# Attention of a two-layer decoder trunk: keys placed by transfers from a shared tile, their product issued earlier, rotated queries' low parts on GpSimd, two weight strips split in halves

## The chip, the core and the metric

The kernel runs on one core of a Trainium2 chip. The metric is the device time of one execution in microseconds (us). Before the change it is 1211.8 us, the median of three runs (1211.34 to 1211.82).

## What is computed

A trunk of two layers over 512 tokens of width 1024, all in float32. Layer 0 mixes tokens by latent attention, layer 1 by an mLSTM; each is followed by a squared-ReLU MLP of width 4096. The change touches only the attention of layer 0:

```
proj = u @ w_in                                   # 512 (c_q) + 256 (c_kv) + 32 (k_r)
q  = rms_norm(c_q, g_q) @ w_uq                    # 16 heads x (64 plain + 32 rotated)
kv = rms_norm(c_kv, g_kv) @ w_ukv                 # 16 heads x (64 keys + 64 values)
q_r, k_r = rope(q_r), rope(k_r)                   # k_r is shared by all heads
for blk in range(4):                              # 128 queries each
    s = (q_n @ k_n.T + q_r @ k_r.T) * 96 ** -0.5  # causal
    p = softmax(s)
    o = p @ v
h = h + o @ w_o
```

## The kernel before

TensorE takes float32 operands as two parts, a high part (a cast to the matmul type, on ScalarE) and a low part (the difference, on VectorE or GpSimd); a product is three matmuls (high x low, high x high, low x high) for each 128 rows of the contraction. Every engine runs a list written by hand, in order, and waits on semaphores; nothing is reordered. So an instruction that waits holds all that stand behind it on its engine.

The attention runs head by head, 0 to 15. Two heads are a pair (their 64 key or query columns fill 128 rows), four are a group (their rotated 32 columns fill 128). `attention(head)` on TensorE is a list of: transposes of the softmax weights of this head (`turn_p(head, b)`, block b of four), scores of the next head (`scores(head + 1, b)`), pieces of products that make the next heads' queries and keys (`rope_product(g)`, `nope_product(pair)`, `k_product(pair)`), and last `weigh(head)`, the product of values and transposed weights. The other engines follow with lists of their own for each head. On ScalarE: `pt_high` (high part of the transposed weights, four), `v_high`, `o_second` (moves half of the head's output), a `split` of a weight strip, `exp(head + 1, b)`. On VectorE: `pt_low` (four), `o_add`, `row_max(head + 1, b)`. The chain of one block is scores, `row_max`, `exp`, `turn_p`, `pt_high`, `pt_low`, `weigh`.

For head `2p + e` the score product reads one key tile (`kh[e]`, `kl[e]`: 64 rows of plain keys of the pair, 64 of rotated keys) and one query tile (`qh[e]`, `ql[e]`). The plain queries of a pair are made in the shared tile `nope_hl` (part of `ul`), the rotated ones of a group in `rope_hl` (parts of `whi[0]` and `wlo[0]`), and `place_q(head)` on SyncE copies rows of both into the query tile of the head by three transfers: 64 plain rows (256 KB, high and low side by side), then twice 32 rotated rows (128 KB). `q_in[e]` counts them. The keys of a pair were not moved so: `k_high` and `k_low` wrote straight from PSUM into the key tiles, 64 rows at a time, two instructions each a pair. `k_product(p)` stood near the end of head `2p - 2`, just ahead of `weigh`; `k_high` and `k_low` at the start of head `2p - 1`, ahead of everything else; and `scores(2p, 0)` comes early in that same head.

Weight strips are loaded by SyncE into two raw tiles in turn, split by ScalarE and then GpSimd (`strip_low`). The first two strips of `w_o` (1 MB each) are split during the last heads, in one instruction of 128 x 2048 on ScalarE.

## Time and profile before

| | before |
|---|---|
| median of 3 runs | 1211.8 us |
| the profiled execution, its own time | 1211.47 us |
| its span from the first to the last instruction | 1209.6 us |
| mean granted TensorE clock | 0.995 of full |
| TensorE matmul busy | 1183.6 us, 98% of the span |
| VectorE, ScalarE, GpSimd busy | 605.1, 456.7, 268.6 us |
| share of TensorE in the chain that ended last | 92% |

The attention with its preparation of the first heads lies between 60 and 225 us from the start of the span. A page row of a group of instructions gives its line, engine, operation, tiles, count, busy time and mean. In a timeline, the number in brackets is the time that the engine stood idle before the row, and after the arrow what ended it. The heads begin on TensorE at 82.5 us (head 0) and then about every 8.8 us.

### The profile page before, as it was taken

How to read it: one execution, taken by the hardware profiler on the slowest of the kernel's cores; microseconds unless marked ns; L12 is line 12 of the kernel's file. 1: busy time of each engine (PE TensorE's matmuls, PEld its weight loads, DVE VectorE, ACT ScalarE, POOL GpSimd, SP SyncE). 2: the span in 40 equal slices, each digit the busy share in tenths (PEclk: the TensorE clock that was granted, in tenths of full speed). 3: DMA queues.
4: the chain of work that ended last, by engine and by line, in shares of the span. 5: the costliest groups of instructions: out<-in, count | busy, mean ns of one | idle time of the engine just before them, and what ended most of it. 6: DMA issues, size and time to landing. Idle time of an engine off the chain costs nothing.

```text
span 1209.6 us, 15485 instructions
## 1 busy us (share of the span) xinstructions
PE 1183.6 (98%) x6010; PEld 999.8 (83%) x6010; DVE 605.1 (50%) x825; ACT 456.7 (38%) x707; POOL 268.6 (22%) x247
## 2 busy tenths in 40 slices
PE   9988988999999999999999999999999999999998
PEld 8877777888888888888889899988888888888887
DVE  6756776555334334344457545656543443433432
ACT  6557777533212222122434255634321221222233
POOL 2322223242002002012212145634210110210212
PEclk9999999999999999999999999999999999999999
DMA  7235343232333323322323534413233233332221
GB/s 207 47 78 114 80 118 105 71 104 70 105 105 103 98 79 104 104 89 85 107 70 105 149 92 99 116 36 105 70 105 105 78 101 101 104 104 84 90 74 70
DMA packets 129033, 115.81 MB, mean 96 GB/s; under 512 B 30822, under 2 KB 125252, under 8 KB 128972
## 3 DMA queue, kind: packets, MB, share of 16 engines
q1 hardware_dynamic: 128940, 114.96, 32.2%
q8 instruction: 42, 0.69, 0.2%
q14 instruction: 19, 0.16, 0.0%
q10 hardware_dynamic: 32, 0.01, 0.0%
HBM read 104.45 MB, written 2.11 MB: 88 GB/s over the span
## 4 chain that ended last, share of the span: by engine, by line
PE 92%; DVE 3%; ACT 3%; issue 1%; DMA 0%; POOL 0%; SPq 0%; POOLq 0%; DVEq 0%; ACTq 0%
PE ps L1810 26%; PE ps L1812 26%; PE ps L1811 26%; PE ps L1992 1%; PE ps L2292 1%; PE ps L1938 1%; PE ps L1981 1%; PE ps L2294 1%; PE ps L1939 1%; PE ps L1940 1%; PE ps L2293 1%; PE ps L2003 1%; PE ps L1982 1%; PE ps L2006 1%; PE ps L1983 1%
## 5 line engine op out<-in xcount | busy, mean ns | idle before, releaser
L867 ACT CAST whi<-raw 128x2048 fp32r<-128x2048 f32 (+4 forms) x102 | 176.5, 1732 | 259.0 <-PE ps L1812 246.1
L1304 DVE TENSOR_TENSOR wlo<-raw,whi 128x2048 fp32r<-128x2048 f32 (+2 forms) x88 | 196.9, 2239 | 151.6 <-ACT whi L867 151.6
L1810 PE MATMUL ps<-xl,whi 128*128 128x512 f32 x616 | 242.3, 393 | 0.1
L1812 PE MATMUL ps<-xh,wlo 128*128 128x512 f32 x616 | 239.8, 389 | 0.0
L1811 PE MATMUL ps<-xh,whi 128*128 128x512 f32 x616 | 239.7, 389 | 0.0
L1810 PE MATMUL ps<-ul,whi 128*128 128x512 f32 x560 | 218.5, 390 | 0.3 <-DVE wlo L1304 0.3
L1812 PE MATMUL ps<-uh,wlo 128*128 128x512 f32 x560 | 217.9, 389 | 0.0
L1811 PE MATMUL ps<-uh,whi 128*128 128x512 f32 x560 | 217.8, 389 | 0.0
L775 POOL TENSOR_TENSOR ul<-sq,uh 128x512 fp32r<-128x512 f32 x64 | 83.6, 1307 | 521.2 <-ACT uh L1151 521.2
L1558 DVE TENSOR_TENSOR h<-ps,h 128x512 f32<-128x512 f32 x78 | 53.6, 689 | 176.7 <-PE ps L1812 171.0
L1151 ACT CAST uh<-sq 128x512 fp32r<-128x512 f32 x64 | 39.7, 621 | 266.3 <-DVE sq L1590 266.3
L1810 PEld LDWEIGHTS ps<-xl,whi 128*128 128x128 f32 x616 | 115.7, 188 | 25.2 <-issue 1.6
L1811 PEld LDWEIGHTS ps<-xh,whi 128*128 128x128 f32 x616 | 115.7, 188 | 24.8 <-issue 1.2
L1812 PEld LDWEIGHTS ps<-xh,wlo 128*128 128x128 f32 x616 | 115.6, 188 | 24.1
L1810 PEld LDWEIGHTS ps<-ul,whi 128*128 128x128 f32 x560 | 105.1, 188 | 22.3 <-DVE wlo L1304 0.7
L1812 PEld LDWEIGHTS ps<-uh,wlo 128*128 128x128 f32 x560 | 105.1, 188 | 21.9
L1811 PEld LDWEIGHTS ps<-uh,whi 128*128 128x128 f32 x560 | 105.2, 188 | 21.6
L1584 DVE TENSOR_TENSOR diag<-ps,r_a 128x512 f32<-128x512 f32 x64 | 44.1, 688 | 105.6 <-PE ps L1812 105.5
L709 POOL TENSOR_TENSOR acc<-acc,sq 128x512 f32<-128x512 f32 x30 | 48.8, 1627 | 129.3 <-ACT sq L881 128.8
L1810 PE MATMUL ps<-wlo,xh 128*128 128x256 f32 x256 | 73.6, 287 | 0.0
L1811 PE MATMUL ps<-whi,xh 128*128 128x256 f32 x256 | 72.4, 283 | 0.0
L1812 PE MATMUL ps<-whi,xl 128*128 128x256 f32 x256 | 72.4, 283 | 0.0
(293 smaller groups left out, 1679.9 us busy)
## 6 DMA issues: line engine op xcount, KB each, us to landing
raw<-in_mlp_w SPq DMA_DIRECT2D x64, 1024.0 KB, 5.3
raw<-in_mlstm_w_in SPq DMA_DIRECT2D x12, 1024.0 KB, 5.3
raw<-in_mla_w_o SPq DMA_DIRECT2D x4, 1024.0 KB, 5.1
raw<-in_mlstm_w_o SPq DMA_DIRECT2D x4, 1024.0 KB, 5.2
raw<-in_mla_w_uq SPq DMA_DIRECT2D x48, 64.0 KB, 2.2
x_tok<-in_x SPq DMA_DIRECT2D x4, 512.0 KB, 7.0
raw<-in_mla_w_in SPq DMA_DIRECT2D x2, 1024.0 KB, 5.7
xh<-ul SPq DMA_DIRECT2D x8, 256.0 KB, 3.0
```

The costliest lines, as they stand in the source:

```text
L709: g.tensor_tensor(acc[:], acc[:], sq[:, k % 2, :], ALU.add).then_inc(acc_add, 1)
L775: g.tensor_tensor(ul[:, j, :], sq[:, j % 2, :], uh[:, j, :].bitcast(F32), ALU.subtract) \
L867: last = sc.copy(hi, src)
L1151: sc.copy(uh[:, m, :], sq[:, m % 2, :]).then_inc(u_hi, 1)
L1304: last = v.tensor_tensor(lo, src, hi.bitcast(F32), ALU.subtract)
L1558: return v.tensor_tensor(h[:, m, :], bank(t % RING), h[:, m, :], ALU.add)
L1584: v.tensor_tensor(diag[:, m % 2, :], bank((t0 + m) % RING), r_a[:], ALU.mult) \
L1810: mm(o, ah, bl, start=first, stop=False)
L1811: mm(o, ah, bh, start=False, stop=False)
L1812: ins = mm(o, al, bh, start=False, stop=last)
L1938: mm(bank(b), wh[:, k, :], cql[:, k, :], start=(k == 0), stop=False)
L1939: mm(bank(b), wh[:, k, :], cqh[:, k, :], start=False, stop=False)
```

## The change

- The keys of pairs 1 to 7 go through a shared tile `k_hl` (in the upper half of `raw[0]`): one cast and one subtraction of 128 x 512 in place of two of 64 x 512 each, then `place_k(p, e)`, a transfer of 64 rows x 4 KB (256 KB) for each head, counted by `k_in[e]`. `k_product(p)` moves from the end to the top of head `2p - 2`, that of pair 1 ahead of `scores(0, 0)`; the cast (`k_staged`) and the subtraction (`k_staged_low`) now stand in that head too.
- On SyncE `place_k(p, 0)` stands ahead of `place_q(2p)` and `place_q(2p + 1)`, and `place_k(p, 1)` behind them.
- The plain queries of pair 0 are written straight into the query tiles (two casts, two subtractions of 64 x 512), so `place_q(0)` and `place_q(1)` are two transfers each, and each waits for its own part of the rotation.
- The low parts of the rotated queries of groups 1 to 3 (two of 128 x 512 a group) move from VectorE to GpSimd.
- On ScalarE `v_high` moves behind `pt_high(head, 1)`, `rope_high` behind `exp(head + 1, 0)`, `o_high` from even to odd heads, `rows_spread` ahead of `exp(head + 1, 2)`.
- On TensorE, pieces of the rotated and plain query products are spread otherwise: heads 2, 6 and 10 get a piece in the middle; the last plain query product ends in head 11, not in head 12.
- The first two strips of `w_o` are split in halves of 128 x 1024, one in each of heads 12 to 15. The load of the second now stands behind the last placement and waits for the landing of the keys.

```diff
+            def place_k(p, e):
+                rows = slice(64 * e, 64 * e + 64)
+                sp.wait_ge(k_lo, k_count(p))
+                sp.wait_ge(s_mm, 4 * (2 * p - 2 + e) + 4)
+                sp.dma_start(k_in_place[e][rows, :, :].bitcast(F32), k_hl[rows, :, :].bitcast(F32)).then_inc(k_in[e], 16)
...
             for g in range(1, GROUPS):
                 load_z(g)
+                place_k(2 * g - 1, 0)
                 place_q(4 * g - 2)
                 place_q(4 * g - 1)
+                place_k(2 * g - 1, 1)
                 load_x(g + 1)
...
+                place_k(2 * g, 0)
                 place_q(4 * g)
                 place_q(4 * g + 1)
-            load(N_WO + 1, cols(a["mla_w_o"][0], 256))
+                place_k(2 * g, 1)
+            place_k(PAIRS - 1, 0)
             place_q(HEADS - 2)
             place_q(HEADS - 1)
+            place_k(PAIRS - 1, 1)
+            for e in range(2):
+                sp.wait_ge(k_in[e], 16 * (PAIRS - 1))
+            load(N_WO + 1, cols(a["mla_w_o"][0], 256))
...
+            def k_staged(p):
+                act.wait_ge(k_mm, p + 1)
+                for e in range(2) if p > 1 else ():
+                    act.wait_ge(k_in[e], 16 * (p - 1))
+                sc.copy(k_hl[:, 0, :], bank(B_KV)).then_inc(k_hi, 1)
...
+            def k_staged_low(p):
+                dve.wait_ge(k_hi, 2 + p)
+                low(k_hl[:, 1, :], bank(B_KV), k_hl[:, 0, :]).then_inc(k_lo, 1)
...
                 if b == 0:
-                    pe.wait_ge(q_in[e], 48 * (head // 2 + 1))
-                    pe.wait_ge(k_lo, head + 1)
+                    pe.wait_ge(q_in[e], q_count(head))
+                    pe.wait_ge(*((k_in[e], 16 * (head // 2)) if head >= 2 else (k_lo, head + 1)))
...
+                if head and part % 2 == 0 and head // 2 + 1 < PAIRS:
+                    k_product(head // 2 + 1)
...
                 if head % 2:
                     spread_scales(head // 2)
-                elif head // 2 + 1 < PAIRS:
-                    k_product(head // 2 + 1)
                 weigh(head)
```

Three places in the engines' lists. First SyncE's queue, where heads 4 and 5 are served (`whi` and `wlo` hold the rotated parts, `ul` the plain ones, `raw` the new key tile). Before:

```order
L587 DMA xh<-ul 64x1024 [waits rope_lo,n_lo,s_mm]
L590 DMA xh<-whi 32x1024
L590 DMA xh<-wlo 32x1024
L587 DMA xl<-ul 64x1024 [waits rope_lo,n_lo,s_mm]
L590 DMA xl<-whi 32x1024
L590 DMA xl<-wlo 32x1024
```

And now:

```order
L619 DMA xh<-raw 64x1024 [waits s_mm,k_lo]
L607 DMA xh<-ul 64x1024 [waits n_lo,s_mm]
L611 DMA xh<-whi 32x1024 [waits rope_lo]
L611 DMA xh<-wlo 32x1024 [waits rope_lo]
L607 DMA xl<-ul 64x1024 [waits n_lo,s_mm]
L611 DMA xl<-whi 32x1024 [waits rope_lo]
L611 DMA xl<-wlo 32x1024 [waits rope_lo]
L619 DMA xl<-raw 64x1024 [waits s_mm,k_lo]
```

The transfer of keys, which waits for the keys' low part, now heads the queue of query transfers.

Second ScalarE in head 2, from the first cast of transposed weights to the third and fourth (`xh` rows with `t_mm` are `pt_high`, `vhl` is `v_high`, `o_part` is `o_second`, `rope_raw` is read by `rope_high`). Before:

```order
L1003 CAST vhl<-v_all 128x4x2x64 [waits w_mm]
L996 CAST xh<-ps 128x128 [waits t_mm,w_mm]
L996 CAST xh<-ps 128x2x128 [waits t_mm]
L1011 COPY o_part<-ps 64x512 [waits w_mm]
L971 CAST whi<-rope_raw 128x512 [waits rope_new,q_in1,q_in0]
L971 CAST wlo<-rope_raw 128x512 [waits rope_new]
L986 ACTIVATE prob,rsum<-ps,nmax 128x128 [waits t_mm,s_max]
L996 CAST xh<-ps 128x3x128 [waits t_mm]
L996 CAST xh<-ps 128x4x128 [waits t_mm]
```

And now:

```order
L1057 CAST xh<-ps 128x128 [waits t_mm,w_mm]
L1057 CAST xh<-ps 128x2x128 [waits t_mm]
L1064 CAST vhl<-v_all 128x4x2x64 [waits w_mm]
L1072 COPY o_part<-ps 64x512 [waits w_mm]
L1047 ACTIVATE prob,rsum<-ps,nmax 128x128 [waits t_mm,s_max]
L1027 CAST whi<-rope_raw 128x512 [waits rope_new,q_in1,q_in0]
L1027 CAST wlo<-rope_raw 128x512 [waits rope_new]
L1012 CAST raw<-ps 128x512 [waits k_in1,k_in0,k_mm]
L1057 CAST xh<-ps 128x3x128 [waits t_mm]
L1057 CAST xh<-ps 128x4x128 [waits t_mm]
```

The value cast now stands behind the first two weight casts, and the rotation's casts and the keys' cast stand between the first exponential and the last two weight casts.

Third TensorE between the end of head 2's scores for head 3 and its `weigh` (`pt` and `vhl` products are `weigh`, `ckvl`/`ckvh` are the key product). Before:

```order
L1984 MATMUL ps<-maskr,identr 128x128
L1810 MATMUL ps<-ckvl,whi 128x512 [waits r_ready,k_lo,wlo_ready]
L1811 MATMUL ps<-ckvh,whi 128x512
L1812 MATMUL ps<-ckvh,wlo 128x512
L1810 MATMUL ps<-ckvl,whi 128x512
L1811 MATMUL ps<-ckvh,whi 128x512
L1812 MATMUL ps<-ckvh,wlo 128x512
L2003 MATMUL ps<-xh,vhl 128x512 [waits o_sum,v_lo,t_hi]
```

And now:

```order
L2054 MATMUL ps<-maskr,identr 128x128
L2073 MATMUL ps<-xh,vhl 128x512 [waits o_sum,v_lo,t_hi]
L2073 MATMUL ps<-xh,vhl 128x384
L2073 MATMUL ps<-xh,vhl 128x256
L2073 MATMUL ps<-xh,vhl 128x128
L2076 MATMUL ps<-xl,vhl 128x512 [waits t_lo]
```

The key product no longer stands between the last scores and `weigh`; it is at the head's top, ahead of the first transpose.

## Rows read from the trace of the kernel before

**Rows 1.** Who TensorE waited for, in total: us, times, longest.

```profile
PE ps L1981 <- DVE xl L1309: 6.1, 4, 3.0
PE ps L1981 <- ACT prob L986: 4.8, 4, 1.4
PE ps L1992 <- DVE xl L1309: 3.6, 4, 1.6
PE ps L1981 <- DMA xh<-wlo: 3.1, 1, 3.1
...
PE ps L1992 <- DVE pt_b L1309: 0.6, 1, 0.6
```

**Rows 2.** Three stretches: length, busy us (PE, PEld, DVE, ACT, POOL), clock, DMA share, GB/s.

```profile
78.50:82.50 4.00, 3.95 (x17) 3.66 (x17) 1.27 (x3) 1.69 (x6) 0.00 (x0) 0.58 0.76 173
176.40:182.00 5.60, 4.07 (x22) 3.37 (x22) 4.51 (x11) 4.58 (x13) 1.26 (x1) 1.00 0.79 187
201.10:206.00 4.90, 4.74 (x22) 4.22 (x23) 3.58 (x8) 2.92 (x10) 0.01 (x1) 0.65 0.77 237
```

**Rows 3.** TensorE's timeline: start us, length, line, operation, idle before it.

```profile
78.55 0.33 PE L1981 MATMUL ps<-xl,xh 128*128 128x128 f32 x1 [3.09 <-DMA xh<-wlo]
...
99.76 0.50 PE L1992 MATMUL ps<-ident,prob 128*128 128x128 f32 x3
...
106.55 0.45 PE L1810 MATMUL ps<-ckvl,whi 128*128 128x512 f32 x1
...
107.99 0.75 PE L2003 MATMUL ps<-xh,vhl 128*128 128x512 f32 x4
...
111.25 0.30 PE L1981 MATMUL ps<-xl,xh 128*128 128x128 f32 x1 [0.78 <-DVE xl L1309]
...
117.87 0.44 PE L1938 MATMUL ps<-cql,whi 128*128 128x512 f32 x1
...
128.58 0.30 PE L1981 MATMUL ps<-xl,xh 128*128 128x128 f32 x1
...
181.98 0.30 PE L1981 MATMUL ps<-xl,xh 128*128 128x128 f32 x1 [1.51 <-DVE xl L1309]
...
201.12 0.30 PE L1981 MATMUL ps<-xl,xh 128*128 128x128 f32 x1 [3.04 <-DVE xl L1309]
```

**Rows 4.** ScalarE's timeline in head 2.

```profile
101.10 0.62 ACT L1003 CAST vhl<-v_all 128x512 fp32r<-128x512 f32 x1
101.62 0.55 ACT L996 CAST xh<-ps 128x128 fp32r<-128x128 f32 x2
102.19 0.58 ACT L1011 COPY o_part<-ps 64x512 f32<-64x512 f32 x1
...
105.18 0.37 ACT L986 ACTIVATE prob<-ps,nmax 128x128 f32<-128x128 f32 x1 [1.25 <-DVE nmax L1471]
...
105.53 0.96 ACT L996 CAST xh<-ps 128x384 fp32r<-128x384 f32 x2
```

**Rows 5.** VectorE's timeline in head 2.

```profile
102.80 0.69 DVE L1496 TENSOR_TENSOR diag<-ps,o_part 64x512 f32<-64x512 f32 x1 [0.18 <-ACT o_part L1011]
...
104.85 0.29 DVE L1471 TENSOR_REDUCE nmax<-ps 128x1 f32<-128x128 f32 x1
...
106.04 0.56 DVE L1309 TENSOR_TENSOR xl<-ps,xh 128x384 fp32r<-128x384 f32 x1 [0.89 <-ACT xh L996]
...
106.84 0.68 DVE L1309 TENSOR_TENSOR xl<-ps,xh 128x512 fp32r<-128x512 f32 x1
```

**Rows 6.** GpSimd's timeline in head 3.

```profile
109.98 1.27 POOL L753 TENSOR_TENSOR ul<-diag,uh 128x512 fp32r<-128x512 f32 x1 [6.91 <-ACT uh L1016]
```

**Rows 7.** SyncE's queue at the first placement: start us, length of issue.

```profile
74.03 0.54 SPq L587 DMA_DIRECT2D xh<-ul  x1
...
75.26 0.61 SPq L590 DMA_DIRECT2D xh<-wlo  x1
```

**Rows 8.** The line of the rotated parts' transfers: issue to landing.

```profile
DMA to landing us min/median/max: 2.9/3.2/4.4
```

More of the change, by code:

```diff
@@ L242, in trunk @@
         ptl = [xl[:, 0:TT, :], pt_b[1][:, :, :]]
-        kh = [xh[:, 4 + e, :] for e in range(2)]
-        kl = [xl[:, 4 + e, :] for e in range(2)]
+        k_in_place = [xh[:, 4:6, :], xl[:, 4:6, :]]
+        kh = [t[:, 0, :] for t in k_in_place]
+        kl = [t[:, 1, :] for t in k_in_place]
+        k_hl = raw[0][:, 1024:2048].bitcast(F32R).rearrange("p (c s) -> p c s", c=2)
         q_in_place = [xh[:, 6:8, :], xl[:, 6:8, :]]
@@ L390, in trunk @@
         q_in = [sem(f"q_in{e}") for e in range(2)]
+        k_in = [sem(f"k_in{e}") for e in range(2)]
+        out_hi, out_lo = sem("out_hi"), sem("out_lo")
         k_mm, k_hi, k_lo = sem("k_mm"), sem("k_hi"), sem("k_lo")
@@ L862, in split @@
                 if n >= 2:
-                    which, value = strip_over(n - 2, gemm_done, n_mm, k_mm)
+                    which, value = strip_over(n - 2, gemm_done, n_mm, k_mm, rope_mm)
                     act.wait_ge(which, i * over + value)
@@ L973, in nope_high @@
             def nope_high(p):
-                for e in range(2) if p else ():
-                    act.wait_ge(q_in[e], 48 * p)
                 act.wait_ge(n_mm, p + 1)
+                if p == 0:
+                    for e in range(2):
+                        rows = slice(64 * e, 64 * e + 64)
+                        sc.copy(qh[e][rows, :], ps[rows, n_bank(0), :]).then_inc(n_hi, 1)
+                    return
+                for e in range(2) if p > 1 else ():
+                    act.wait_ge(q_in[e], q_count(2 * p - 2))
                 sc.copy(nope_hl[:, 0, :], bank(n_bank(p))).then_inc(n_hi, 1)
@@ L1057, in attention @@
                 nxt = head + 1 < HEADS
+                pt_high(head, 0)
+                pt_high(head, 1)
                 if not second:
                     v_high(i)
-                elif nxt:
-                    for e in range(2):
-                        k_high(e, i + 1)
-                pt_high(head, 0)
-                pt_high(head, 1)
                 if head:
                     o_second(head - 1)
-                if head % 4 != 2 and head + 3 < HEADS:
-                    n = split_at(head)
-                    split(n, "full" if n >= N_WO else head_strip(n))
-                elif head % 4 == 2 and head + 2 < HEADS:
-                    rope_high(head // 4 + 1)
+                if head >= HEADS - 4:
+                    out_high((head - HEADS + 4) // 2, second)
+                elif head % 4 != 2:
+                    split(split_at(head), head_strip(split_at(head)))
                 if nxt:
@@ L1075, in attention @@
                     nope_high(nope_at[head])
+                elif head % 4 == 2 and head + 2 < HEADS:
+                    rope_high(head // 4 + 1)
+                if not second and head and i + 1 < PAIRS:
+                    k_staged(i + 1)
                 if second:
@@ L1081, in attention @@
                     exp(head + 1, 1)
+                if second:
+                    rows_spread(i)
                 if nxt:
@@ L1084, in attention @@
                     exp(head + 1, 3)
-                if i and not second:
+                if i and second:
                     o_high(i - 1)
-                if second:
-                    rows_spread(i)
-                if head + 2 == HEADS:
-                    split(N_WO + 1)
             for head in range(HEADS):
@@ L1464, in nope_low @@
             def nope_low(p):
-                dve.wait_ge(n_hi, p + 1)
+                dve.wait_ge(n_hi, p + 2 if p else 2)
+                if p == 0:
+                    for e in range(2):
+                        rows = slice(64 * e, 64 * e + 64)
+                        last = low(ql[e][rows, :], ps[rows, n_bank(0), :], qh[e][rows, :])
+                    last.then_inc(n_lo, 1)
+                    return
                 low(nope_hl[:, 1, :], bank(n_bank(p)), nope_hl[:, 0, :]).then_inc(n_lo, 1)
@@ L1518, in attention @@
                     row_scales(i)
-                if second and nxt:
-                    for e in range(2):
-                        k_low(e, i + 1)
                 pt_low(head, 0)
@@ L1526, in attention @@
                 turning = head % 4 == 0 and head + 4 < HEADS
-                if head % 4 == 2 and head + 2 < HEADS:
-                    rope_low(head // 4 + 1)
                 if nxt:
@@ L1539, in attention @@
                     rope_table(head // 4 + 1, 1)
+                if not second and head and i + 1 < PAIRS:
+                    k_staged_low(i + 1)
                 pt_low(head, 3)
@@ L2048, in _ @@
             nope_product(1, range(4))
+            k_product(1)
             for b in range(TT):
```

117 lines of the change are left out of this document (70 added, 47 removed).

## The prediction, made before the changed kernel was run

> **What bounds the kernel now.** I read the busy shares first, then the list of TensorE's waits, then TensorE's timeline head by head, and beside it those of ScalarE, VectorE, GpSimd and SyncE in the same stretches. The busy share says that TensorE sets the time: 98% of the span. The change adds or removes no matmul, so it can only move what TensorE lacks, its waits and the clock behind them. The list puts nearly all of that in the attention: 6.1 + 4.8 + 3.6 + 3.1 + 0.6 = 18.2 us [rows 1]. Two of these waits are long: 3.09 us ahead of the very first scores, for the placing of queries, and 3.04 us ahead of head 14's scores, for the keys' low part [rows 3]. The granted clock fell behind both, to 0.58 over 4.0 us and to 0.65 over 4.9 us [rows 2], which is 4.0 x 0.42 and 4.9 x 0.35, 1.7 us each. Behind the waits of the third group (up to 1.6 us) it stayed at 1.00 [rows 2]. So about 21.6 us could be won at most. The reader should also see the rhythm: head 2 starts at 99.76, the scores of head 4 at 111.25, head 4 at 117.87, the scores of head 6 at 128.58 [rows 3]. I call the start of an even head T and the first scores of the next pair, inside the odd head, S. Before, T to S is 11.5 us in head 2 and 10.7 us in head 4; S to the next T is 6.6 us.
>
> **The start.** Only the rotated parts are now transferred for heads 0 and 1, and they no longer stand behind the plain low part (a subtraction of 0.68 us like that of [rows 5]). The last one was issued at 75.26 [rows 7]; without the plain transfer and the rest between it and the first (1.23) and without that subtraction it goes out at about 73.3 and lands 3.2 us later [rows 8], at 76.5. Meanwhile TensorE does pair 1's key product (107.99 - 106.55 = 1.44 us, [rows 3]), which ends at about 76.8. So the scores start 1.8 us sooner with 1.4 us more done, and the fall of the clock goes (1.7): 4.9 us. Against it: the keys' cast and subtraction of pair 1 now stand ahead of the first maximum, and the fourth block of scores waits about 0.7 for the first exponential; and in head 0 the last low part of the weights stands behind both rotation tables and the plain low part, so that `weigh` and the placing for head 2 come some 1.6 us later against the matmuls. Net gain by the scores of head 2: 2.6 us.
>
> **Even heads 2, 6, 10.** The new chain runs key product, cast, subtraction, four transfers, scores, and T to S is its length: 1.44 for the product; 0.3 until the first transpose can be copied (an estimate from the 0.50 us that three take, [rows 3]); on ScalarE 0.57 for two weight casts (101.62 to 102.19), 0.52 for the value cast, which now stands behind them (101.10 to 101.62), 0.61 for the moved output half until VectorE adds (102.19 to 102.80) [rows 4, 5]; 0.69 for the add, 0.33 maximum (104.85 to 105.18), 0.35 exponential (105.18 to 105.53) [rows 4, 5]; two rotation casts 1.05 and the keys' cast 0.52 (each like the value cast of 128 x 512); 0.51 until the third weight block is subtracted (105.53 to 106.04), 0.80 for that and the next maximum (106.04 to 106.84), 0.68 for the keys' subtraction (the same shape, [rows 5]). That is 8.4 us from T. SyncE needs 0.1 to see it, 0.54 for the keys' transfer, 1.23 from the plain queries' issue to that of the last rotated part [rows 7], and 3.2 to land [rows 8]: S = T + 13.4, against 11.5: **+1.9 us each, three times 5.7**. Queries that have long been ready stand behind the keys in SyncE's queue, with those of the next head behind them in turn.
>
> **Even heads 4 and 8.** Here a further piece of product (0.7) stands at the top, and VectorE has two rotation tables in the list, the second ahead of the keys' subtraction. Product and piece 2.1; as above to the exponential 3.0 and 0.35; keys' cast 0.5, handover 0.5, subtraction and maximum 0.8, table 0.6, keys 0.7: 8.6 from T. With the same 5.1 for SyncE and landing, S = T + 13.7 against 10.7: **+2.9 or 3.0 each, together 5.8**. Before, the queries of these heads had been placed a head earlier.
>
> **Head 12.** It starts at 181.98 + 6.6 = 188.6 and S is 201.12, 12.5 us [rows 3]. Now there is no rotation, only the half strip beside the add: 7.3 + 5.1 = 12.4, -0.1. Its scores keep a wait of nearly 3 us and the fall of the clock. Behind it TensorE has a piece of 0.7 less to do than before, since that stood in front already, and the 0.6 us that the 128 x 2048 cast cost in head 15 goes [rows 1]: -1.3. The second strip's load, now behind the keys' landing, goes out about 15 us after T, and ScalarE wants it some 6 us later; a strip has four times the bytes of a keys' transfer. I cost it at nothing, and at 1 to 2 if it is late.
>
> **Costed at nothing.** Casts and subtractions saved (one each a pair, two subtractions a group on VectorE) free engines that wait in these stretches anyhow. GpSimd's two low parts of 1.27 us [rows 6] end 6.6 us after the first transpose, 0.3 us before the keys' subtraction would (7.0), and 2 us before the last transfer asks: hidden. If that cover went, each microsecond would be paid in each of three groups. `k_product` no longer stands between the last scores and `weigh`; the weights' low part now comes about 1 us late there, but that wait lies inside T to S and is not added.
>
> **Sum**: -2.6 + 5.7 + 5.8 - 0.1 - 1.3 = +7.5 us. Then the clock. In heads 3, 7 and 11 TensorE is ready for the scores 10.7 after T (keys' subtraction 8.4, last weights 0.7, second half of `weigh` 0.6, a piece 0.7, transposes 0.3), so it stands still for 2.7 us; in heads 5 and 9 for 2.1. Waits of 3.0 and 3.1 lowered the clock, one of 1.5 did not [rows 2, 3]; I take the row that it is nearest to and charge 1.7 for each of the three, 5.1, and nothing for the two. +12.6 on the profiled execution's own 1211.47 (span 1209.6; the median of the runs, 1211.8, is 0.3 above): **1224 us**.
>
> **Bounds.** No fall of the clock at all, in head 13 neither: 7.5 - 1.7 = +5.8, and with the shortest landing (2.9, six times 0.3) +4.0: 1215.5. The other way, the keys' 256 KB lie ahead of the queries in the transfer engines, which moved 237 GB/s in the busiest stretch [rows 2], so they take 1.1 us and not the 0.54 of their issue: 6 x 0.6 = 3.6, and the clock falls behind the two waits of 2.1 as well (3.4): 1231.
>
> A rule against the trace: the Trainium skill, DMA: Bandwidth & Descriptors, "Anatomy of one DMA", fits a transfer (issued by GpSimd) as about 2.0 us plus bytes over 436 GB/s. For 128 KB that is an estimate of 2.3 us; this trace shows 3.2 [rows 8] and does not agree. By the page the sum would be 6 x 0.9 = 5.4 less.
>
> **The rivals.** (a) Forecast, placement late: 0.63, 1224, its own range 1215 to 1231. (b) Placement lands in time, **faster**: my chain of thirteen steps is too long, because ScalarE and VectorE overlap more than the old rows show. Then the first wait (2.6), the wait in head 13 with its clock (4.7) and the end (1.3) are won, and the groups stay where they are: 1203. It decides where T to S is 2 to 3 us shorter than I have it, that is 11.5 and 10.7; break-even, without falls of the clock, is at about 1 us a pair. For it: before, the queries' six transfers were in time (the wait for head 4's scores ended with VectorE, [rows 3]). Against it: none of them had to follow a product of the same head. 0.22. (c) The landings are shorter than the rows (2.3 instead of 3.2), the waits 1.8 and the clock stays up: 7.5 - 5.4 - 1.7 = +0.4, 1211.9, **no change**. 0.10. Its figure is that of the DMA page above; the trace speaks against it. (d) GpSimd is the late one: its rotated low parts start 4.0 after the first transpose and the last transfer can go out at 8.8, so from 2.4 us each they hold it; at 2.9 each it is 1 us in each of three groups: 1227. 0.05. The Trainium skill, GPSIMD Engine Reference, "Key points", says that GpSimd shares its SBUF interfaces with VectorE and contends with instructions of two SBUF inputs; in this trace the operation took 1.27 against VectorE's 0.68, and no row shows it longer at 128 x 512.
>
> **How the numbers follow.** A measurement of this kernel tells about 0.2% (2.4 us) from no change. Slower: (a), (d) and a little of (c): 0.70. Same: most of (c): 0.07. Faster: (b): 0.23. The range goes from 1205, which takes in the near part of (b), to 1231; it leaves out the rest of (b), 0.15, and little above.
>
> **What would show it.** TensorE's first wait shrinks to well under 1 us and the clock stays near 1.00 there; that step would be right even if the total is not. In heads 3, 7 and 11 a wait of 2 to 3.5 us ahead of the first scores, ended by a transfer into `xh` from `wlo`, and a shorter one in 5 and 9; 13 to 14 us from T to S; the granted clock near 0.6 behind the longer ones. Keys' transfers issued 8 to 9 us after T. The prediction is wrong if those waits are under 1 us, if they end with VectorE, or if a strip or GpSimd ends them.

## The result and the profile after

The changed kernel takes 1233.5 us (median of four runs, 1232.49 to 1235.56); its ratio to the kernel before is 1.0175, interval 1.0153 to 1.0198. It is slower, as forecast, but by more: 1224 was forecast, with 1231 as the upper end. The profiled execution has a span of 1233.4 us against 1209.6, so 23.8 us are to be found in the trace. It is the slowest of the four (1235.6 us, granted clock 0.985 against 0.987 and 0.988), so spans that are compared with it below overstate a difference of medians by about 2 us.

Who TensorE waited for (us, times, longest), which answers to [rows 1]:

```profile
PE ps L2051 <- DMA xh<-wlo: 9.2, 3, 3.4
PE ps L2051 <- issue: 8.1, 4, 3.1
PE ps L2076 <- DVE xl L1369: 5.4, 7, 0.9
PE ps L2073 <- ACT xh L1057: 4.4, 4, 1.4
PE ps L2051 <- ACT prob L1047: 1.7, 5, 0.6
```

L2051 is the first matmul of `scores`. "Issue" names nothing, but these four waits stand at the same place and end as the last rotated part lands. The long waits of before are gone, and six new ones stand ahead of the first scores of heads 4 to 14. L2076 and L2073 are the two halves of `weigh`.

TensorE's timeline, answering to [rows 3]: T is the first row of a key product (L1878), S the first scores of a pair.

```profile
79.16 0.50 PE L2051 MATMUL ps<-xh 128*128 128x512 f32 x1 [0.60 <-ACT prob L1047]
...
90.39 0.30 PE L2051 MATMUL ps<-xh 128*128 128x128 f32 x1 [0.33 <-issue]
...
97.02 0.44 PE L1878 MATMUL ps<-ckvl,whi 128*128 128x512 f32 x1
...
104.47 0.85 PE L2073 MATMUL ps<-xh,vhl 128*128 128x512 f32 x4 [1.36 <-ACT xh L1057]
...
106.10 0.85 PE L2076 MATMUL ps<-xl,vhl 128*128 128x512 f32 x4 [0.78 <-DVE xl L1369]
...
111.34 0.45 PE L2051 MATMUL ps<-xh 128*128 128x128 f32 x1 [2.63 <-DMA xh<-wlo]
...
120.77 0.44 PE L1878 MATMUL ps<-ckvl,whi 128*128 128x512 f32 x1
...
135.24 0.30 PE L2051 MATMUL ps<-xh 128*128 128x128 f32 x1 [2.50 <-issue]
...
141.87 0.44 PE L1878 MATMUL ps<-ckvl,whi 128*128 128x512 f32 x1
...
156.18 0.45 PE L2051 MATMUL ps<-xh 128*128 128x128 f32 x1 [2.21 <-issue]
...
165.40 0.45 PE L1878 MATMUL ps<-ckvl,whi 128*128 128x512 f32 x1
...
180.49 0.30 PE L2051 MATMUL ps<-xh 128*128 128x128 f32 x1 [3.11 <-issue]
...
188.72 0.44 PE L1878 MATMUL ps<-ckvl,whi 128*128 128x512 f32 x1
...
203.12 0.45 PE L2051 MATMUL ps<-xh 128*128 128x128 f32 x1 [3.39 <-DMA xh<-wlo]
...
212.73 0.45 PE L1878 MATMUL ps<-ckvl,whi 128*128 128x512 f32 x1
...
225.88 0.30 PE L2051 MATMUL ps<-xh 128*128 128x128 f32 x1 [3.17 <-DMA xh<-wlo]
```

S of head 2 comes 2.75 us sooner than before (93.14). From there to S of head 14 it is 135.5 us against 108.0, 27.5 more. Behind it lie 1007.5 us against 1008.5, 1.0 less. The sum is 23.8. In those 135.5 us T to S takes 14.3, 14.5, 14.3, 15.1, 14.4 and 13.2 us, and S to the next T takes 6.6, 9.4, 6.6, 9.2, 8.2 and 9.6. The differences in the second list are the clock's, as the windows show (length, busy of PE, PEld, DVE, ACT, POOL, granted clock, DMA share, GB/s; [rows 2] are those of before):

```profile
78.50:82.50 4.00, 3.40 (x21) 2.83 (x20) 2.19 (x6) 3.03 (x11) 0.00 (x0) 1.00 0.57 115
106.00:111.30 5.30, 2.62 (x10) 1.83 (x10) 3.64 (x10) 3.33 (x8) 0.76 (x1) 0.61 0.89 196
111.30:115.00 3.70, 3.66 (x11) 2.91 (x12) 0.29 (x1) 0.46 (x2) 1.04 (x1) 0.50 0.84 195
135.20:139.00 3.80, 3.76 (x26) 3.42 (x27) 0.65 (x2) 1.90 (x6) 0.43 (x1) 1.00 0.89 175
```

Behind the very first scores the clock is now 1.00. In head 3 it is at its lower level, 1.2 of 2.4 GHz, from about 107.1 us on, ahead of the long wait, which begins at 108.7, and through the 3.7 us behind S to about 117.4. In head 7 it was low from about 151.5 and the long wait began at 154.0. In head 5, behind a wait of 2.50 us, it did not fall at all.

SyncE's queue for heads 4 and 5 (start, length of issue), answering to [rows 7]:

```profile
105.47 0.50 SPq L619 DMA_DIRECT2D xh<-raw  x1
106.07 0.54 SPq L607 DMA_DIRECT2D xh<-ul  x1
106.67 0.60 SPq L611 DMA_DIRECT2D xh<-whi  x1
107.32 1.26 SPq L611 DMA_DIRECT2D xh<-wlo  x1
```

The keys' transfer leaves at T + 8.45, the last rotated part at T + 10.3; the scores that wait for it start 4.0 us after that issue. Issue to landing, median, of this transfer in the changed kernel:

```profile
xh<-wlo SPq DMA_DIRECT2D x8, 128.0 KB, 3.9
```

GpSimd's two low parts in head 2:

```profile
102.62 1.28 POOL L788 TENSOR_TENSOR whi<-rope_raw,whi 128x512 fp32r<-128x512 f32 x1 [1.37 <-ACT whi L1027]
103.85 1.29 POOL L788 TENSOR_TENSOR wlo<-rope_raw,wlo 128x512 fp32r<-128x512 f32 x1
```

They end at 105.14, 0.3 us ahead of the keys' transfer and 1.5 ahead of the first transfer that waits for them, so they held nothing. But the rotated queries for head 4 had been ready for only 0.3 us when the keys' transfer left; the plain ones had long been.

### The profile page after: what moved, and what is told of

Same layout as the page of the kernel before. It is cut to its first block, busy times and chain, and to the rows that moved or that the text cites. A ratio compares the mean times of both kernels' runs of the same rounds, so it can differ in the third digit from the quotient of the medians.

```text
span 1233.4 us, 15493 instructions
## 1 busy us (share of the span) xinstructions
PE 1196.3 (97%) x6010; PEld 1008.7 (82%) x6010; DVE 597.0 (48%) x813; ACT 455.1 (37%) x703; POOL 276.7 (22%) x253
## 4 chain that ended last, share of the span: by engine, by line
PE 91%; ACT 3%; DVE 2%; issue 2%; DMA 1%; SPq 0%; POOL 0%; POOLq 0%; DVEq 0%; ACTq 0%
PE ps L1878 26%; PE ps L1880 25%; PE ps L1879 25%; PE ps L2062 1%; DMA xh<-wlo 1%; PE ps L2006 1%; PE ps L2361 1%; PE ps L2008 1%; PE ps L2007 1%; PE ps L2363 1%; PE ps L2362 1%; PE ps L2076 1%; PE ps L2051 1%; PE ps L2212 1%; PE ps L2210 1%
## 5 line engine op out<-in xcount | busy, mean ns | idle before, releaser
L911 ACT CAST whi<-raw 128x2048 fp32r<-128x2048 f32 (+4 forms) x100 | 172.6, 1728 | 259.0 <-PE ps L1880 246.1
L1878 PE MATMUL ps<-xl,whi 128*128 128x512 f32 x616 | 242.3, 393 | 0.1
L1878 PE MATMUL ps<-ul,whi 128*128 128x512 f32 x560 | 218.5, 390 | 0.3 <-DVE wlo L1364 0.3
L1878 PEld LDWEIGHTS ps<-xl,whi 128*128 128x128 f32 x616 | 115.7, 188 | 25.3 <-issue 1.6
L1878 PEld LDWEIGHTS ps<-ul,whi 128*128 128x128 f32 x560 | 105.1, 188 | 22.3 <-DVE wlo L1364 0.7
L1878 PE MATMUL ps<-wlo,xh 128*128 128x256 f32 x256 | 73.5, 287 | 0.0
```

The costliest lines, as they stand in the source:

```text
L911: last = sc.copy(hi, src)
L1878: mm(o, ah, bl, start=first, stop=False)
```

## The experiments

The kernel before had a median of 1210.6 us beside the first four runs, 1211.8 beside the next four, 1211.3 beside the third four and 1211.8 beside the last three; where two kernels of different groups are compared, the difference of the ratios, times 1211.8, is given. For the runs that bear on the clock, this table gives what each profile shows: the waits ahead of S in heads 3, 5, 7, 9 and 11, and behind them the time from S to the first scores in the next even head. At full clock that stretch is 9.0, 8.3, 9.0, 8.3 and 8.3. A fall of the clock that ended ahead of S doesn't show in this table. The intervals of the ratios are 1 to 4 us to either side, so differences of 1 or 2 us between kernels are not clear of noise by the ratios alone.

| kernel | waits ahead of S | S to the next even head's first scores |
|---|---|---|
| changed | 2.6, 2.5, 2.2, 3.1, 3.4 | 11.8, 8.3, 11.6, 9.9, 11.3 |
| filled | none | 9.0, 8.3, 9.0, 8.3, 8.3 |
| filled_short | 1.3, 0.5, 1.3, 1.2, 1.4 | 10.6, 8.3, 10.6, 8.3, 9.9 |
| filled_fit | 0.2, 0.2, 0, 0, 1.1 | 9.1, 8.3, 9.0, 8.3, 11.3 |
| scores_filled | none | 9.0, 8.3, 9.0, 8.3, 8.3 |
| weigh_filled | 3.4, 2.5, 3.4, 3.1, 3.4 | 10.6, 9.9, 11.7, 8.3, 9.9 |
| cast_late | 4.5, 3.7, 4.6, 3.7, 4.5 | 10.6, 9.9, 11.7, 11.0, 11.1 |
| keys_half | 2.7, 1.8, 1.2, 2.5, 2.6 | 10.6, 8.3, 9.0, 9.9, 9.9 |

**q_first: the queries' first transfers ahead of the keys' in SyncE's queue.** For all pairs:

```
-                place_k(2 * g, 0)
                 place_q(4 * g)
+                place_k(2 * g, 0)
                 place_q(4 * g + 1)
```

> The changed kernel with one thing reordered on SyncE: each head's query transfers are issued ahead of its keys' transfer, not behind it. Theory A (the keys' transfer, last link of the new chain, holds ready queries behind it, and the long wait also lowers the clock): only one transfer follows the keys' subtraction, so the first scores of a pair come about 2.4 us sooner in six places, 14 us, and the waits get short enough that the clock mostly stays up, another 6 to 10: 1209 to 1214. Theory B (the 768 KB a head are limited by the transfer engines, in whatever order): the scores gain under 1 us each and the clock still falls: 1227 to 1232.

Measured: 1212.5 us, ratio 1.0013 (1.0001 to 1.0024). Swapping two entries of one queue takes 19.6 us off (0.0162 x 1211.8). It lies in the range of the first theory. From the even head's first scores to S it is now 9.0 to 10.5 us in place of 11.5 to 12.7, 14.7 us less over the six heads, and no stretch behind S is long; the rest is the clock. In heads 5, 9 and 13 the queries left 8 us or more ahead of the keys. In heads 3, 7 and 11 the rotated parts waited for GpSimd's low parts instead; counted from the same start they left 2.7 and 2.2 us sooner in head 3 (at 104.68 and 105.92). The placing now lies almost wholly beside other work. The waits for it that are left, the landing of the rotated part, and a stretch in head 2 of which more is said below:

```profile
PE ps L2051 <- DMA xh<-raw: 2.1, 2, 1.4
...
xh<-wlo SPq DMA_DIRECT2D x8, 128.0 KB, 2.6
...
106.86 1.43 PE L2076 MATMUL ps<-xl,vhl 128*128 128x512 f32 x4 [0.78 <-DVE xl L1369]
...
106.00:110.00 4.00, 3.23 (x13) 2.65 (x12) 3.01 (x8) 1.60 (x7) 0.00 (x0) 0.57 0.82 188
```

**filled: TensorE kept busy in its waits.** 40 matmuls of 128 columns ahead of the first scores of heads 4 to 14, 22 ahead of `weigh` in heads 2, 6 and 10; their results are overwritten.

```
+                if head % 2 and head > 1:
+                    pe.wait_ge(k_lo, k_count((head + 1) // 2))
+                    for _ in range(40):
+                        mm(ps[:, B_KV, 0:P], identr[:], maskr[:], start=True, stop=True)
                 scores(head + 1, 0)
...
+                elif part == 2:
+                    pe.wait_ge(o_sum, head)
+                    for _ in range(22):
+                        mm(ps[:, B_PV, 0:P], identr[:], maskr[:], start=True, stop=True)
                 weigh(head)
```

> The changed kernel with matmuls of 128 columns that nobody reads put into its waits: 40 ahead of the first scores of heads 4, 6, ... 14 (about 2.2 us at full clock), 22 ahead of the weighing of heads 2, 6, 10. The work is the same otherwise, and the waits last as long. Theory A (a third to a half of the loss is the clock behind the waits): the clock stays near 1.0 and the time falls by 8 to 11 us, to 1223 to 1226. Theory B (all of it is waiting, the clock costs 1 or 2): 1231 to 1234, or slower by what the extra matmuls overrun.

Measured: 1230.9 us, ratio 1.0168 (1.0151 to 1.0185). The fillers were longer than the waits: a pitch of 0.11 us, as the row shows (start, length, count behind the x), so that S came 6.7 us late in sum over six heads. What they kept off was more: the clock was 1.00 throughout, as the first theory said, and the span is 4.7 us shorter. So the clock had cost 4.7 + 6.7 = 11.4 us in the profile of the changed kernel. The time lies at the edge of the second theory's range: by the ratios only 0.8 us was won, which is not clear of noise.

```profile
107.99 4.66 PE L2142 MATMUL ps<-maskr,identr 128*128 128x128 f32 x40
```

**direct_early and direct_late: the keys written directly again.** Casts and subtractions of 64 x 512 into the key tiles at the start of the odd head, as before the change, and no `place_k`. In the first the key products stay at the top of the even heads; in the second those of pairs 2 to 7 go back ahead of `weigh`. The rest of the change stays.

```
-                place_k(2 * g, 0)
                 place_q(4 * g)
                 place_q(4 * g + 1)
-                place_k(2 * g, 1)
...
+                if second and nxt:
+                    for e in range(2):
+                        k_high(e, i + 1)
                 pt_high(head, 0)
```

> The changed kernel with the keys' part undone: high and low parts of keys are written straight from PSUM into the key tiles at the start of odd heads, as before the change; the key product stays at the top of even heads. Theory A: no scores wait for a transfer; only the start's gain, the waits of the weighing in even heads (about 1 us each) and VectorE's low parts ahead of the odd heads' scores remain: 1203 to 1209. Theory B (the rest of the change, the rotated low parts on GpSimd or the reordered casts, costs as well): above 1214.

> As the kernel direct_early, but with the key products of pairs 2 to 7 back between the last scores and the weighing of even heads. Theory A: the product covers the wait for the weights' low part, 0.5 to 1 us in each of six even heads: 2 to 5 us below direct_early, 1200 to 1205. If the early product by itself is worth something (it gives ScalarE and VectorE time to catch up at the top of the head), direct_late is equal to or slower than direct_early.

Measured: 1204.3 us (0.9948; 0.9932 to 0.9965) and 1200.1 us (0.9912; 0.9896 to 0.9929). Both lie in the range of their first theory. By the ratios the transfers of keys, with their casts and subtractions in the even head, cost 27.5 us (0.0227) and the early product 4.4 (0.0036); all the rest of the change is worth 10.7 (0.0088) on the other side. In direct_late S of head 2 stands at 90.04, that of head 14 at 192.40, and the span is 1198.4: against the rows of before, 3.1 us won by S of head 2, 2.7 to S of head 12, 2.9 to S of head 14 (the wait of 3.04 became 0.32), 2.5 behind it, where the clock no longer fell. Its longest waits:

```profile
PE ps L2045 <- DVE xh L1363: 4.7, 5, 1.3
PE ps L2056 <- DVE xl L1363: 2.3, 4, 1.1
PE ps L2045 <- ACT prob L1041: 2.2, 4, 0.6
```

**filled_short, filled_fit, scores_filled, weigh_filled: how much is the clock's, and whose waits lower it.** The edit is that of filled with other numbers. filled_short has 18 and 12; filled_fit has 29 (22 in head 5) and 12; scores_filled only those 29 and 22, weigh_filled only the 12.

```
-                    for _ in range(40):
+                    for _ in range(22 if head == 5 else 29):
```

> The changed kernel, with matmuls of 128 columns into banks that are then overwritten, put into TensorE's waits so that it does not stand idle: 18 ahead of the first scores of heads 4, 6, 8, 10, 12 and 14 (at the 0.11 us apiece that the run with 40 showed: 2.0 us, less than the waits of 2.2 to 3.4) and 12 ahead of the weigh of heads 2, 6 and 10 (1.3 us, the length of the wait there). Nothing is left out of the computation. Theory A, the clock is a large part of the loss: with waits left that are under 1.4 us the clock stays near 1.00, the stretch from the first scores to the end of the odd head takes 6.6 us in place of 9.4, and the first scores stand where they stood (111.3 in the first group): 2 to 2.8 us won behind five or six of them, 1220 to 1224. Theory B, the run with 40 gained little because the clock costs little and the waits are all: 1232 to 1234.

> The changed kernel with filling matmuls of 128 columns, whose results are overwritten, fitted to the waits that the runs with 40 and with 18 left: 29 ahead of the first scores of heads 4, 8, 10, 12 and 14, 22 ahead of head 6, 12 ahead of the weigh of heads 2, 6 and 10. Nothing of the computation is left out. Theory A: the fall of the clock behind the waits of 2.2 to 3.4 us costs what its rows say, 2.8 us behind each of the waits in heads 3, 7, 9, 11 and 13 or so; with the waits filled the clock is 1.00 throughout, every first scores keeps its place after the start of the even head, and the kernel takes 1220 to 1224. Theory B: the clock that is seen low is a matter of how the matmuls behind a wait are fed, and filling it changes nothing: 1231 to 1234.

> The changed kernel with filling matmuls only in the waits ahead of the first scores (29 in heads 3, 7, 9, 11 and 13, 22 in head 5; results overwritten); the waits ahead of weigh stay empty. Theory A, the waits ahead of weigh lower the clock by themselves, late in the even head: the stretch behind the first scores in heads 3, 7 and 11 is 10.6 us or the low clock stands in the fillers, and the kernel takes 1228 to 1232. Theory B, waits of 1.4 and 0.8 us cost no clock of their own: with the long ones filled the stretches are 9.0 us as in the run with 40 matmuls, and the kernel takes 1222 to 1226.

> The changed kernel with filling matmuls only in the waits ahead of the weigh of heads 2, 6 and 10 (12 of 128 columns, 1.3 us, results overwritten); the waits ahead of the first scores stay empty. Theory A, the waits of 1.36 and 0.78 us in the even head make the clock fall sooner and stay low longer behind the placement wait: with the first of them filled, the first scores keep their place (14.4 us after the even head's start), and the stretch from there to the first scores of the next even head, 11.6 to 11.8 us in heads 3, 7 and 11 of the changed kernel and 9.0 at full clock, comes down to 10.6: 3 to 4 us in all, 1229.5 to 1231. Theory B, only the placement wait next to it sets the loss: the stretches stay at 11.6 to 11.8, 1233.

Measured: 1231.0 us (1.0151; 1.0132 to 1.0170), 1230.5 (1.0150; 1.0126 to 1.0173; single runs from 1226.8 to 1233.2), 1227.2 (1.0122; 1.0105 to 1.0139) and 1233.7 (1.0179; 1.0162 to 1.0196). The first three lie between their two theories, weigh_filled at its second. In scores_filled only the long waits are filled, and the short ones ahead of `weigh` stay (4.4 and 5.4 us in its list, as in the changed kernel). In head 2 they cost no clock; in heads 6, 10 and 12 it fell right behind them and was back before S:

```profile
104.00:106.00 2.00, 0.85 (x4) 0.66 (x4) 2.00 (x5) 0.88 (x3) 1.04 (x1) 1.00 0.00 0
106.00:112.00 6.00, 5.89 (x45) 5.50 (x46) 3.45 (x10) 3.22 (x8) 1.82 (x1) 1.00 0.91 210
112.00:119.00 7.00, 7.00 (x43) 6.06 (x42) 3.34 (x7) 4.86 (x14) 0.00 (x0) 1.00 0.41 86
...
148.00:152.00 4.00, 3.94 (x16) 3.46 (x17) 2.54 (x8) 2.07 (x7) 0.00 (x0) 0.57 0.88 181
192.00:195.50 3.50, 3.50 (x14) 3.06 (x15) 2.43 (x8) 2.07 (x7) 0.00 (x0) 0.56 0.86 178
213.00:216.50 3.50, 3.34 (x12) 2.85 (x13) 2.31 (x7) 1.59 (x5) 0.00 (x0) 0.52 0.80 171
```

In these three places S came 1.3, 1.2 and 1.3 us late, and in the other three in its place: this is the price of three falls for which there was no long wait, as the first theory of this run had it. q_first shows the same. Its heads 2, 6 and 10 have the short waits (1.36 and 0.78 us) and no long one behind them, and the clock fell right behind the second each time, to 0.57 or 0.58 over 4 us (for head 2 see its rows above). In direct_early, where the two waits are 0.87 and 0.18, it never fell.

The span of scores_filled is 7.9 us shorter than that of the changed kernel (6.4 by the ratios). With the 3.8 us that it still paid, the clock had cost 11.7, which agrees with the 11.4 of filled: the table's 10.0 by head 11 and 1.6 behind the scores of head 14, where the clock fell in the kernel before too. filled_fit shows that a wait of 1.1 us that is left, with the fillers just ahead of it, can cost 3 us of clock, and filled_short that one of 1.3 costs 1.6 and one of 1.2 nothing. (That wait is there because the last rotated part took 5.0 us from issue to scores in this head, against 4.1 in the changed kernel; why is not known.) weigh_filled was to show whether the short waits deepen the fall: head 3 came down from 11.8 to 10.6 as that theory had it, head 11 from 11.3 to 9.9 and head 9 to full clock, but head 7 stayed at 11.7 and head 5 rose to 9.9. The table's cost is 7.5 in place of 10.0, while the median did not move. Neither theory holds head by head.

**keys_half: the keys' transfers cut to 32 rows (128 KB).** The other rows of keys stay those of pair 0.

```
-                rows = slice(64 * e, 64 * e + 64)
+                rows = slice(64 * e, 64 * e + 32)
```

> The changed kernel with the keys' transfers cut from 64 rows to 32, 128 KB in place of 256; the other 32 rows of plain keys stay those of pair 0, so the scores are those of other keys. Theory A, the rotated queries land late (3.7 us and not 3.2) because the keys' 256 KB lie ahead of them in the transfer engines: the landing of the rotated parts comes down to 3.2 to 3.4, each first scores 0.4 to 0.6 sooner, in six heads 3 us, and up to 2 more where the clock falls later: 1228 to 1231. Theory B, the landing is slow for another reason (strips loading, the queue's own pace): landing stays at 3.7, 1232 to 1235.

Measured: 1227.9 us (1.0128; 1.0097 to 1.0160; single runs from 1222.4 to 1230.7). The transfers left when they had (105.46, then 107.30 for the last rotated part), that part's issue took 0.60 us in place of 1.26, and S came at 110.67 in place of 111.34; counted from the even head's first scores it is 0.61 to 0.76 sooner in all six heads, 4.0 us in sum. The scores start 2.8 us after the end of that issue in head 3 of both kernels, and in every other head the two agree to 0.1, so the 0.66 lies in how long the issue took. Of the 9.3 us by which the profiled span is shorter, 5.2 are clock (4.8 in the table against 10.0), and the median lies just under the first theory's range. The edit halves the bytes and the rows alike, so which of the two counts isn't shown. The landing:

```profile
xh<-wlo SPq DMA_DIRECT2D x8, 128.0 KB, 3.2
```

**cast_late: the keys' cast and subtraction behind the last of the weights.** On ScalarE and VectorE alike:

```
-                if not second and head and i + 1 < PAIRS:
-                    k_staged(i + 1)
                 if second:
                     rows_turned(i)
                 pt_high(head, 2)
                 pt_high(head, 3)
+                if not second and head and i + 1 < PAIRS:
+                    k_staged(i + 1)
```

> The changed kernel with the keys' cast moved behind the last two casts of the weights on ScalarE, and the keys' subtraction behind the last subtraction of the weights on VectorE. Theory A: TensorE's waits of 1.36 and 0.8 us ahead of the two halves of weigh lie inside the stretch from the even head's start to the first scores, whose end the keys' chain sets: they go (9.8 us in total become under 4), the keys' transfers leave 0.8 to 1.3 us later, and the waits ahead of the first scores grow by what is saved and this delay: seven pairs by about 1.0 us, 1237 to 1243. Theory B: those waits are themselves on the path, and without them the odd head is reached sooner and the scores with it: 1225 to 1230.

Measured: 1238.1 us (1.0224; 1.0208 to 1.0239). The waits ahead of `weigh` fell from 9.8 to 3.7 us, and the wait for the placing took them over, as the first theory said:

```profile
104.42 0.85 PE L2073 MATMUL ps<-xh,vhl 128*128 128x512 f32 x4 [0.86 <-ACT xh L1057]
105.46 0.85 PE L2076 MATMUL ps<-xl,vhl 128*128 128x512 f32 x4 [0.18 <-DVE xl L1369]
...
111.87 0.38 PE L2051 MATMUL ps<-xh 128*128 128x128 f32 x1 [4.47 <-DMA xh<-wlo]
```

From the even head's first scores to S it is 12.7 us, as in the changed kernel (12.6): the keys' transfer left only 0.1 us later against the matmuls, not the 0.8 to 1.3 expected, since the casts of the weights, now ahead, also let the subtraction of the third block and the maximum go sooner. So the short waits lay inside T to S. The profiled span is 1.8 us longer than that of the changed kernel, 1.3 of it in the last column of the table: more falls of the clock. The medians lie 4.6 us apart: the changed kernel's profile is of an execution 2.1 us above its median, this one's of one 0.7 below.

**split_late and split_early: the two halves of the keys taken apart.** On direct_late the second half goes behind the first weights, and the first half's subtraction ahead of the softmax scales; on direct_early the first half moves to the end of the even head as well.

```
                 if second and nxt:
-                    for e in range(2):
-                        k_high(e, i + 1)
+                    k_high(0, i + 1)
                 pt_high(head, 0)
                 pt_high(head, 1)
+                if second and nxt:
+                    k_high(1, i + 1)
```

> The kernel that writes the keys directly with the product ahead of weigh (1200.13), with the two halves taken apart: the cast and the subtraction of the first head's keys stay at the start of the odd head, the subtraction ahead of the softmax scales; those of the second head's keys, which are needed a head and a half later, stand behind the first two casts and subtractions of the weights. Theory A, TensorE's waits for the keys' subtraction ahead of the first scores (4.7 us, five times) are the length of this chain, which gets 0.5 us shorter on VectorE and 0.6 shorter on each engine for the first weights: 2 to 4 us faster, 1196 to 1198. Theory B, those waits hide others (the first maximum, the last weights), and what is won there is waited for behind: 1199.5 to 1200.5.

> The kernel that writes the keys directly with the product at the top of the even head (1204.27), with the halves taken apart: the first head's keys are cast and subtracted at the end of the even head, behind the last exponential and the last maximum, the second head's behind the first two casts and subtractions of the weights in the odd head. Theory A: the wait for the keys' subtraction (6.8 us, seven times) goes altogether, and some of it comes back at the maximum or the weights: 1198 to 1200. Theory B: the loss of the early product (4.1 us against the late one) is the product itself, which stands ahead of the transposes and delays the exponentials; nothing is changed in that, 1203 to 1204.

Measured: 1203.9 us (0.9933; 0.9919 to 0.9948) and 1210.6 us (0.9988; 0.9979 to 0.9997), 2.5 and 4.8 us slower than what they started from (by the ratios); both theories of both missed. The wait that was to shrink stayed, in split_late at 1.21 of 1.28 us. The reason is on ScalarE: the first half's cast stands behind the last exponential, which ends just ahead of it and sets the chain.

```profile
104.48 0.69 ACT L1041 ACTIVATE prob<-ps,nmax 128x512 f32<-128x512 f32 x1
105.07 0.19 ACT L1041 ACTIVATION_READ_ACCUMULATOR prob<-ps,nmax 128x1 f32 x1
105.16 0.57 ACT L999 CAST xh<-ps 64x512 fp32r<-64x512 f32 x1
```

What the second half took off the start it put ahead of the next maximum, and in split_early `turn_scales` waited 2.5 us, summed over six heads, for its subtraction. That this makes up the whole loss is only argued.

**rope_back, v_first, piece_up: parts of the rest, on direct_late.** rope_back puts the rotated low parts back on VectorE and their casts ahead of the first exponential. piece_up moves a piece of product into the wait of heads 3, 7 and 11. v_first is piece_up with `v_high` ahead of the weights' casts again.

```
-                    nope_product(2 * g + 3, (1,))
+                    nope_product(2 * g + 3, (1, 2))
...
-                    nope_product(2 * g + 3, (2, 3))
+                    nope_product(2 * g + 3, (3,))
```

> The kernel that writes the keys directly with the product ahead of weigh (1200.13), with the rotated queries' low parts back on VectorE, behind the addition of the output halves, and their casts back ahead of the first exponential, as before the change. Theory A: this part of the change is worth what it takes off the way of the first maximum in heads 2, 6 and 10, two subtractions of 0.6 us each on VectorE, of which TensorE has 0.5 us of wait to spare: 1.5 to 3 us slower, 1201.5 to 1203. Theory B: GpSimd's operations of 1.27 us hold up VectorE or the placement as much as they save: 1199.5 to 1200.5.

> The kernel that writes the keys directly with the product ahead of weigh (1200.13), with one more piece of the plain query product (0.7 us) ahead of the transposes in heads 3, 7 and 11 and one less behind the first scores. Theory A: TensorE waits 1.28 us there for the keys' subtraction with nothing else to do, so the piece is hidden in the wait: 1.5 to 2.1 us faster, 1198 to 1198.7. Theory B: the piece delays the transposes, the weights' casts and the exponential behind them, and what is won ahead of the scores is waited for behind: 1199.5 to 1201.

> The fastest kernel so far (keys written directly, product ahead of weigh, one piece of the query product moved up; 1199.43) with the value cast back ahead of the first two casts of the weights in the even heads. Theory A: it stands on the way from the transposes to the first maximum in every even head (0.52 us until the first weights are cast, and the addition is not sooner either), and the waits there are small already: 0 to 2 us slower, 1199.5 to 1201.5. Theory B: GpSimd gets the values' low part 0.5 us sooner and weigh waits for that: 1198.5 to 1199.3.

Measured: rope_back 1202.4 us (0.9928; 0.9914 to 0.9942), 1.9 slower than direct_late by the ratios; piece_up 1199.4 us (0.9903; 0.9888 to 0.9918), 1.1 faster by the ratios, the fastest of all; v_first 1200.3 us (0.9903; 0.9886 to 0.9919), the same as piece_up by the ratio, so ScalarE's new order for `v_high` is worth nothing that shows. In rope_back TensorE waited 6.4 us for exponentials where it had been 2.2, and the profiled span is 2.2 us longer; this part of the change is a gain, though 1.9 us is within what the two ratios' intervals allow. In piece_up the wait for the keys fell from 4.7 to 2.6 us and about half of that came through in the span (1198.4 to 1197.4); waits of 0.7 us in sum for the weights arose behind it.

## Why the prediction was right in its sign and too low in its size

**The start** was right: 2.75 us by S of head 2 against 2.6, the first wait gone, the fourth block waiting 0.60 for the first exponential (0.7), the clock at 1.00.

**The chain of the even heads** was right up to SyncE. The keys' transfers left 8.45 us after T in head 2 and 8.7 in heads 4 and 8 (174.13 - 165.40), against 8.4 and 8.6; the waits stand where they were named. What failed is the last link, "3.2 to land". From issue to scores it was 4.0 in head 2 and 3.9 to 4.5 in the others, because 256 KB of keys are now issued just ahead; the issue itself took 1.26 us in place of about 0.6. The prediction had this as a bound, 0.6 us each; keys_half shows 0.66 for half of the keys' bytes, q_first with no keys ahead a landing of 2.6. The Trainium skill, DMA: Bandwidth & Descriptors, "Queues, rings and completion order", says that each transfer engine takes its descriptors in ring order, so that bytes issued earlier stand ahead; the trace agrees. T to S came out at 85.7 us over the six heads where the terms give 80.0: 5.7 too little, 4.0 of it shown by keys_half. The rest, above all the 4.5 us to S in head 9, was not tried apart. "Queries that have long been ready" held for the plain ones and for heads 6, 10 and 14, but not for the rotated ones of heads 4, 8 and 12. Sending the keys from another engine's queue was not tried either.

**The clock** is the other step that failed: "I charge 1.7 for each of the three, 5.1, and nothing for the two". By head 11 it cost 10.0 us: 2.8, 0, 2.6, 1.6 and 3.0 behind the five waits. Three things were wrong in it. The price of one fall was taken from the kernel before, where it stood alone, and here it was up to 3.0. And a wait's length was taken to decide whether it falls: waits of 2.5 and 3.1 us went free in one profile and cost 1.6 in another, those of 1.1 to 1.4 us cost from nothing to 3. Third, the weights' wait ahead of `weigh` was put aside, since it "lies inside T to S". For the wait itself that holds, but behind two such waits, 1.36 and 0.78 us, the clock fell by itself in q_first and scores_filled, and in heads 3 and 7 of the changed kernel it was down before the long wait began. (The row of the kernel before that was to show no fall behind 1.5 us ends at that wait; behind it, from 182 to 186 us, the trace has 1.00 as well.) The price comes in steps, 0, 1.6 or 2.6 to 3.0; per wait of 2.2 us or more it is 1.5 to 2 us on the mean (10.0 over five in the changed kernel, 7.5 over five in weigh_filled). The Trainium skill, TensorE: Matmul & The Clock Gate, "Part 1: The HAM clock gate", says that the number of slow matmuls at a kernel's start differs from run to run. No run here tries the start, but single runs of filled_fit and keys_half lie 6 and 8 us apart with granted clocks of 0.993 to 0.998 and 0.985 to 0.993.

**The end** was nearly right, 1.0 against 1.3, and the strip's load behind the keys' landing cost nothing. Misses of 5.7 in T to S, 4.9 in the clock and 0.3 at the end, less 0.15 at the start, make 10.8 of the 11.2 us between the forecast 12.6 and the 23.8. The upper end of the range had added 3.6 and 3.4, and neither was enough. It had named the first cause; of the clock it allowed 1.7 us a fall, and only behind the long waits. The profile is 2.1 us above the median, which misses 1224 by 9.5.

**The rivals.** That placement lands in time (1203) is ruled out. That 1204.3 is what the change gives without the transfers is a number near it by another way. Short landings came only where the queries stand first, and there the time is the same as before, 1212.5. GpSimd was not late: in head 2 it ended at 105.14 and the transfer that waits for it left at 106.67. rope_back puts its part as a gain of some 2 us.

## What to carry to other kernels

When work goes through a transfer in place of a direct write, cost what stands behind it in the same queue, in issue order and in bytes: here two swapped entries were worth some 20 us, and the direct write 27. Charge a wait of over a microsecond on TensorE with an expected loss of clock on top, as a chance over steps and not as a threshold on its length, and count shorter waits close together too. And before moving an instruction to shorten a chain, look at what it stands behind: the keys' cast stood behind the last exponential, and moving the halves apart behind it made the kernel slower.

## What the runs showed of the hardware

- Forty identical matmuls of 128 columns in a row have a pitch of 0.11 us, and so have the three matmuls of 128 columns in a first block of scores. That is twice what the single mask of 128 columns behind wider matmuls takes (0.06).
- SyncE's issue of a transfer of 128 KB took 0.60 us with 128 KB of keys ahead and 1.26 with 256 KB, and the transfers behind it left 0.7 us later (108.68 against 108.00).
- Waits of 1.36 and 0.78 us with 0.85 us of work between them were enough for a fall of the clock: behind them it fell in all three heads of q_first that have them, in two of the three in scores_filled, and in two of three in the changed kernel, but not in head 2 of scores_filled. What decides between 0, 1.6 and nearly 3 us stays open.
